# Attention in a decoder layer: the split of the output weights moved from VectorE and GpSimd to GpSimd alone, and spread over two pairs of heads

## The chip, the cores and the metric

The kernel runs on one core of a Trainium2 chip. The metric is the device time of one execution, in microseconds. TensorE is the matrix engine (its matrix products are PE in the profile, its weight loads PEld), VectorE is DVE, ScalarE is ACT, GpSimd is POOL, and SyncE (SP) only issues transfers.

## The reference, cut to what matters

The kernel computes one decoder layer: a projection of a 2048 x 1024 input, a pooling mixer and an attention beside each other, an output projection, and a gated MLP. The part in question is the attention, with 8 heads of width 64 and 16 blocks of 128 queries:

```python
z = jnp.einsum('bhqd,bhkd->bhqk', qi, kf) * scale
causal = key_pos[None, :] < q_pos[:, None]
log_1m_beta = jnp.where(causal, jax.nn.log_sigmoid(-z), 0.0)
stick = lax.cumsum(log_1m_beta, axis=3, reverse=True) - log_1m_beta
a = jnp.where(causal, jnp.exp(jax.nn.log_sigmoid(z) + stick), 0.0)
return jnp.einsum('bhqk,bhkd->bhqd', a, vf)
```

Behind it comes `mix = merged @ w_out[l]`, with `w_out` of 1024 x 1024. That product is made from two halves of each operand: a high half, the float32 value rounded to fp32r, and a low half, the rest. The weights of `w_out` are brought in and split into these halves while attention still runs, for use by the next phase.

## The kernel before, in words

The phases follow each other: values, projections, attention (`phase_attention`, from about 399 to 905 us of the profile), the output projection (`phase_mix`), the two halves of the MLP.

Attention goes over 4 pairs of heads (pair 0 to 3), each with a head 0 and a head 1. A head has 40 units, and a pair so has units 0 to 79. A unit is one block of 128 queries against up to 512 keys; block q has q // 4 + 1 units, and the one on the diagonal, which comes first, is 128, 256, 384 or 512 keys wide. Blocks 0 to 3 are units 0 to 3; units 4 and 5 are block 4, units 6 and 7 block 5, and so on. Pair 0 and pair 3 are written out, pairs 1 and 2 are a loop (`steps`, L628 to L649).

A unit passes through the engines in this way. TensorE makes the scores (`scores`, L887). ScalarE makes `beta` and the remainder from them (L749, L750). VectorE runs a scan over the remainder (L861). GpSimd multiplies `beta` with the scan's result, which gives the weight (L810). TensorE transposes the weight in blocks of 128 (`turn`, L899) and multiplies it with the values (`values`, L913). Each engine has one list of instructions in the order of the units, in which the later stages of a unit stand some steps on: at step u GpSimd makes the product of unit u - 1, TensorE transposes unit u - 4 and multiplies the values of unit u - 6. ScalarE's `beta` of unit u waits for the product of unit u - 4 (four buffers), TensorE's transposition for the product of its own unit, and VectorE's scan of the first unit of block q for the product of the last unit of block q - 2. For units kept in full precision GpSimd also sums the two halves of the values once a head (`sum_v`, L774), ahead of the product of the last unit of block 5 (units 7 and 47).

The output weights come in 16 pieces of 128 x 512 (256 KB), two in flight, into two buffers in `bridge` (`wo_f`, L609). SP issues them (L704 to L707) right after the loads of pair 0's head 1 (`load_head(0, 1)`, L701); from the third on it waits until the piece two before is split (`wo_done`). Each piece has two operations: VectorE copies it to fp32r (`high_wo`, L828 to L832), GpSimd subtracts the copy from the piece (`low_wo`, L769 to L772). `wo_part` (L673) says at which unit that happens: in pair 0 at units 40, 42, 44 and so on to 70, so in head 1. At such a step the piece stands first on both engines.

SP's list goes on only behind the 16th piece: then come the waits for the stores of the projections (`qk_out`), and then, for each head that ends, the loads of the head that will take its buffers (seven transfers, 4 MB) and the two stores of its result (L710 to L714). All transfers of this phase go through SP's queue.

Of the kernel before, what the change touches and what calls it, by code (L numbers as in the profile page):

```python
# [312 lines left out]
def head_loads(s, tiles, heads, tiles_of, pair, e):  # L313

    q_hi, q_lo, k_both, v_both = tiles_of
    half = slice(e * HEAD_DIM, (e + 1) * HEAD_DIM)
    moves = []
    for part in range(2):
        rows = slice(part * HEAD_DIM, (part + 1) * HEAD_DIM)
        moves.append((as_f32(k_both[rows, :]), s["qk"][pair + heads // 2, part, half, :]))  # L320
        for hi_lo, to in enumerate((q_hi, q_lo)):
            moves.append((as_f32(to[rows, :]), s["qk"][pair, hi_lo, half, :]))
    moves.append((as_f32(v_both[:, :, :, :]), s["v"][pair * 2 + e]))
    return moves
# [237 lines left out]
def phase_attention(nc, a, c, s, wide, bridge, retired, first_head, qk_out, mixed_out, mix_start):  # L562
# [8 lines left out]
    heads = a["d_attn"] // HEAD_DIM  # L571
    scale = HEAD_DIM ** -0.5
    lead = 8
# [6 lines left out]
    total = len(units)  # L580
    per_head = total // 2
# [5 lines left out]
    whole_before = [sum(whole[:u]) for u in range(total + 1)]  # L587
    per_pair_halved, per_pair_whole = halved_before[total], whole_before[total]
    v_sum_at = {next(u for u, x in enumerate(units) if x[0] == e and x[1] == per + 1 and x[5]): e for e in range(2)}
    with ExitStack() as stack:  # L590
# [18 lines left out]
        wo_f = bridge[:, 0:2, :]  # L609
# [8 lines left out]
        one_done, wo_hi_done, wo_done = (n.sem(x) for x in ("one_done", "wo_hi_done", "wo_done"))  # L618
        wo_in = n.sems("wo_in", 2)
# [5 lines left out]
        pairs, loads = heads // 2, 7  # L625
# [46 lines left out]

        def wo_part(i, u):  # L673

            m = (u - per_head) // 2
            return m if isinstance(i, int) and i == 0 and (u - per_head) % 2 == 0 and 0 <= m < 2 * a["kc"] else None

        with nc.Block() as block:

            @block.sync  # L680
            def _(sp):
                for sem in mixed_out:
                    sp.sem_inc(sem, 16)

                def load_head(pair, e):
                    for to, source in head_loads(s, tiles, heads, (q_hi[e], q_lo[e], k_both[e], v_both[e]), pair, e):
                        sp.dma_start(to, source).then_inc(head_in[e], 16)

                def store_head(pair, e, first=0, end=tiles):
                    sp.wait_ge(o_read, done((pair * 2 + e) * tiles + (end - 1), lead))  # L690
                    row, cols = (pair * 2 + e) * HEAD_DIM, slice(first * P, end * P)
                    sp.dma_start(s["merged"][bass.ds(a["d_pool"] + row, HEAD_DIM), cols], mixed[e][0:HEAD_DIM, cols]).then_inc(mixed_out[e], 16)
                    sp.dma_start(s["attn_low"][bass.ds(row, HEAD_DIM), cols], mixed[e][HEAD_DIM:P, cols]).then_inc(mixed_out[e], 16)

                def load_first_merged(t):
                    cols = slice(t * P, (t + 1) * P)
                    sp.dma_start(mix_start["low"][t], s["attn_low"].rearrange("(c p) t -> p c t", p=P)[:, :, cols]).then_inc(merged_in[t], 16)
                    sp.dma_start(mix_start["merged"][t], s["merged"].rearrange("(c p) t -> p c t", p=P)[:, :, cols]).then_inc(merged_in[t], 16)

                sp.sem_inc(head_in[0], 16 * loads)  # L700
                load_head(0, 1)  # L701
                for sem in retired:
                    sp.sem_clear(sem)
                for m in range(2 * a["kc"]):  # L704
                    if m >= 2:
                        sp.wait_ge(wo_done, m - 1)
                    sp.dma_start(wo_f[:, m % 2, :], wo_rows[m // 2][:, (m % 2) * BANK:(m % 2 + 1) * BANK]).then_inc(wo_in[m % 2], 16)  # L707
                for e in range(2):
                    sp.wait_ge(qk_out[e], stored(2 * (a["d_attn"] // P) * (seq // BANK) // 2, 32))
                with sp.Fori(0, heads // 2 - 1) as i:  # L710
                    for e in range(2):
                        sp.wait_ge(pv_whole_done, i * per_pair_whole + (whole_before[(e + 1) * per_head] + lead))
                        load_head(i + 1, e)
                        store_head(i, e)  # L714
                store_head(pairs - 1, 0)

                store_head(pairs - 1, 1, 0, 2)
                for e in range(2):
                    sp.wait_ge(mixed_out[e], stored(pairs, 32))
                sp.wait_ge(pv_done, halved(pairs - 1, per_head) + lead)  # L720
                sp.wait_ge(pv_whole_done, kept_whole(pairs - 1, per_head) + lead)
                for t in range(2):
                    load_first_merged(t)
                store_head(pairs - 1, 1, 2, tiles - 2)
                store_head(pairs - 1, 1, tiles - 2, tiles)
# [39 lines left out]
            @block.gpsimd  # L765
            def _(pool):
                pool.sem_inc(weight_done, lead)

                def low_wo(m):  # L769
                    k, h = m // 2, m % 2  # L770
                    pool.wait_ge(wo_hi_done, m + 1)
                    pool.tensor_tensor(wide[2 + h][:, k, :], wo_f[:, h, :], as_f32(wide[h][:, k, :]), ALU.subtract).then_inc(wo_done, 1)  # L772

                def sum_v(pair, e):  # L774

                    pool.wait_ge(head_in[e], 16 * loads * pair + 16 * loads)
                    before = whole_before[e * per_head]
                    if not isinstance(pair, int):
                        pool.wait_ge(pv_whole_done, pair * per_pair_whole + (before + lead))
                    elif pair > 0 or e:  # L780
                        pool.wait_ge(pv_whole_done, pair * per_pair_whole + before + lead)
                    pool.tensor_tensor(v_f[:, :, 0, :], as_f32(v_both[e][:, :, 0, :]), as_f32(v_both[e][:, :, 1, :]), ALU.add).then_inc(v_f_done, 1)

                def first_sum(t):
                    pool.wait_ge(merged_in[t], 32)
                    merged = mix_start["merged"][t]
                    pool.tensor_tensor(merged[:, n_pool:, :], merged[:, n_pool:, :], mix_start["low"][t], ALU.add).then_inc(first_whole, 1)

                def first_scale():
                    pool.wait_ge(mix_start["squared"], 1)  # L790
                    merged = mix_start["merged"][0]
                    pool.tensor_tensor(merged, merged, scales.unsqueeze(2).broadcast_to([P, a["kc"], P]), ALU.mult).then_inc(first_scaled, 1)

                def step(i, u, behind):
                    if in_last_head(i, u) in SUMS_AT:
                        first_sum(SUMS_AT.index(in_last_head(i, u)))
                    if in_last_head(i, u) == SCALE_AT:
                        first_scale()
                    if wo_part(i, u) is not None:
                        low_wo(wo_part(i, u))  # L800
                    if behind(weight_lag):
                        v, t = behind(weight_lag)
                        e, q, key, w, first, _ = units[v]
                        if v in v_sum_at:
                            sum_v(i if u >= weight_lag else i - 1, v_sum_at[v])
                        pool.wait_ge(beta_done, done(t, lead))
                        pool.wait_ge(stick_done, done(t, lead))
                        pool.wait_ge(turned, freed(t, weight_ring, lead))
                        at = col(q, key) + 1
                        pool.tensor_tensor(weight[v % weight_ring][:, 0:w], beta[v % stick_in][:, 0:w], stick[q % 2][:, at:at + w],  # L810
                                           ALU.mult).then_inc(weight_done, 1)

                steps(pool, step)

            @block.vector
            def _(dve):
# [8 lines left out]
                    dve.wait_ge(first_hi_done, 1)  # L825
                    dve.tensor_tensor(mix_start["lo"], mix_start["merged"][0], as_f32(mix_start["hi"]), ALU.subtract)

                def high_wo(m):  # L828

                    k, h = m // 2, m % 2  # L830
                    dve.wait_ge(wo_in[h], 16 * (k + 1))
                    dve.tensor_copy(wide[h][:, k, :], wo_f[:, h, :]).then_inc(wo_hi_done, 1)  # L832

                def step(i, u, behind):
                    if wo_part(i, u) is not None:
                        high_wo(wo_part(i, u))
                    if behind(lo_lag) and not whole[behind(lo_lag)[0]]:
                        v, t = behind(lo_lag)
                        w, pair, slot = units[v][3], i if u >= lo_lag else i - 1, halved_before[v] % wT_ring
# [4 lines left out]
                    if u < total:  # L844
                        e, q, key, w, first, _ = units[u]
# [20 lines left out]
                    if behind(read_lag) and units[behind(read_lag)[0]][5]:  # L866
                        v, t = behind(read_lag)
                        e, q = units[v][0:2]
# [1604 lines left out]
```

## Time and profile before

| what | value |
|---|---|
| median of 3 runs | 2430.19 us (2427.38 to 2430.77) |
| the profiled execution's own time | 2429.78 us |
| its span, from the first to the last instruction | 2428.0 us |
| mean granted clock of TensorE, as a share of full speed | 0.986 |
| TensorE, VectorE, ScalarE, GpSimd busy over the span | 96%, 74%, 50%, 42% |
| DMA over the span | 324.71 MB, mean 134 GB/s |

All times of rows are from one execution, counted from the first instruction. A row of the order of time has start, duration, engine, line, operation, operands, how many equal ones were merged into it (x4), and in brackets how long the engine had been idle and what released it. In the tables by stretch each engine has its busy time with the count of instructions, PEclk is the share of full clock that TensorE was granted, and the last two columns are the busy share of the DMA engines and GB/s.

### The profile page before, as it was taken

The page shows a single profiled execution, that of the slowest core. Times are in us where ns is not written, and L with a number is a line of the kernel's source. Part 1 is how long each engine was busy: PE and PEld are TensorE (multiplying, and loading weights), DVE is VectorE, ACT ScalarE, POOL GpSimd, SP SyncE. Part 2 cuts the span into 40 slices and gives each one's busy share as a digit, 9 for nine tenths or more (in the row PEclk, how much of TensorE's full clock was granted, in tenths as well). Part 3 has the DMA queues.
Part 4 walks back from the last instruction along what each step waited for, and adds up shares of the span by engine and source line. Part 5 has one row for each costly group of instructions (what it writes and reads, how often), then busy time and mean ns, then how long its engine had stood idle before and what let it go on. Part 6 is the DMA issues. An engine that isn't in the chain of part 4 may idle for free. (4 is left out here: it accounts for less than half of the span.)

```text
span 2428.0 us, 36799 instructions
## 1 busy us (share of the span) xinstructions
PE 2326.3 (96%) x11673; PEld 1948.3 (80%) x11673; DVE 1801.1 (74%) x2126; ACT 1217.8 (50%) x2114; POOL 1018.9 (42%) x758
## 2 busy tenths in 40 slices
PE   8999999989999989996999999989999999999997
PEld 6787887878888888884888888778888878888886
DVE  5434224999999977888999999999999973344575
ACT  4311114879889974555444444544444443342352
POOL 0000002776666653566454555455554521041642
PEclk9999999999999999998999999999999999999999
DMA  6412447153333325777233332633333324455584
GB/s 192 140 47 82 136 130 199 32 138 90 85 90 87 86 64 169 225 220 255 88 108 100 116 102 93 204 110 103 95 108 95 116 95 168 161 176 190 196 307 153
DMA packets 264699, 324.71 MB, mean 134 GB/s; under 512 B 12996, under 2 KB 185980, under 8 KB 259580
## 3 DMA queue, kind: packets, MB, share of 16 engines
q1 hardware_dynamic: 262268, 314.72, 41.8%
q0 software_dynamic: 2304, 8.39, 0.9%
q8 instruction: 69, 1.13, 0.2%
q14 instruction: 58, 0.48, 0.1%
HBM read 213.48 MB, written 109.58 MB: 133 GB/s over the span
## 5 line engine op out<-in xcount | busy, mean ns | idle before, releaser
L810 POOL TENSOR_TENSOR weight<-beta,stick 128x512 f32<-128x512 f32 (+3 forms) x320 | 304.8, 961 | 540.9 <-ACT beta L749 422.7
L2186 DVE SCALAR_TENSOR_TENSOR x<-up_cols,taps,x 128x1024 f32<-128x1024 f32 x174 | 263.9, 1517 | 14.4 <-ACT x L2083 11.4
L861 DVE TENSOR_TENSOR_SCAN stick<-z_ps,stick,beta 128x512 f32<-128x512 f32 x192 | 245.1, 1277 | 13.3 <-ACT z_ps L750 12.1
L535 PE MATMUL out_ps<-hT,w_hi 128*128 128x512 f32 x768 | 239.5, 393 | 2.4 <-DVEq L462 2.4
L2173 DVE TENSOR_TENSOR wu_lo<-wu_sums,wu_hi 128x512 fp32r<-128x512 f32 x175 | 213.3, 1219 | 0.0
L749 ACT ACTIVATE beta<-z_ps 128x512 f32<-128x512 f32 (+3 forms) x320 | 171.4, 536 | 57.5 <-PE z_ps L893 50.4
L2070 ACT ACTIVATE wu_hi<-wu_sums 128x512 fp32r<-128x512 f32 x175 | 109.5, 627 | 161.1 <-PE gate_odd_ps L2316 89.5
L2316 PE MATMUL value_chain_ps<-wide,wu_hi 128*128 128x512 f32 x528 | 177.0, 389 | 2.1 <-DVE up_cols L2208 2.1
L910 PE MATMUL wT_ps<-ident,weight 128*128 128x128 f32 x1088 | 173.3, 275 | 3.1 <-POOL weight L810 3.1
L535 PEld LDWEIGHTS out_ps<-hT,w_hi 128*128 128x128 f32 x768 | 145.0, 189 | 34.6 <-DVEq L462 2.8
L750 ACT ACTIVATE z_ps<-z_ps 128x512 f32<-128x512 f32 (+3 forms) x320 | 172.1, 538 | 0.0
L910 PEld LDWEIGHTS wT_ps<-ident,weight 128*128 128x128 f32 x1088 | 135.4, 141 | 32.0 <-POOL weight L810 4.8
L535 PE MATMUL out_ps<-hT,w_lo 128*128 128x512 f32 x384 | 150.2, 391 | 0.0
L2083 ACT ACTIVATE x<-up_cols,taps 128x1024 f32<-128x1024 f32 x87 | 108.4, 1246 | 78.7 <-DVE up_cols L2280 57.4
L1709 DVE TENSOR_TENSOR down_lo<-down_lo,down_hi 128x1024 fp32r<-128x1024 f32 (+1 forms) x57 | 71.7, 1264 | 95.1 <-ACT down_hi L1627 95.1
L1798 PE MATMUL down_ps<-down_hi 128*128 128x512 f32 x352 | 137.2, 390 | 1.6 <-DVE down_lo L1715 1.6
L2316 PE MATMUL value_chain_ps<-wide,wu_lo 128*128 128x512 f32 x352 | 137.0, 389 | 0.0
L1798 PE MATMUL down_ps<-down_hi,down_lo 128*128 128x512 f32 x352 | 136.9, 389 | 0.0
L1798 PE MATMUL down_ps<-down_lo,down_hi 128*128 128x512 f32 x352 | 136.9, 389 | 0.0
L921 PE MATMUL o_ps<-wT_f,v_f 128*128 128x128 f32 x1024 | 136.1, 276 | 0.0
L921 PEld LDWEIGHTS o_ps<-wT_f,v_f 128*128 128x128 f32 x1024 | 125.3, 193 | 0.0
L2316 PE MATMUL value_chain_ps<-x_t,wu_hi 128*128 128x512 f32 x352 | 111.0, 397 | 13.0 <-DVE up_cols L2287 13.0
(279 smaller groups left out, 6205.4 us busy)
## 6 DMA issues: line engine op xcount, KB each, us to landing
wu_f<-in_w_up SPq DMA_DIRECT2D x44, 512.0 KB, 4.9
bridge<-in_w_up SPq DMA_DIRECT2D x44, 512.0 KB, 5.0
f_scratch<-f_sum SPq DMA_DIRECT2D x88, 256.0 KB, 2.0
down_lo<-f_scratch SPq DMA_DIRECT2D x44, 512.0 KB, 3.4
f_scratch<-x SPq DMA_DIRECT2D x66, 256.0 KB, 2.1
down_b<-in_w_down SPq DMA_DIRECT2D x65, 256.0 KB, 3.9
x_scratch<-x SPq DMA_DIRECT2D x56, 256.0 KB, 2.8
first_head<-qk_scratch SPq DMA_DIRECT2D x24, 512.0 KB, 10.0
```

What stands on the lines that cost most here:

```text
L535: m = pe.matmul(out_ps[half + j][:, :], w[slot][:, k, :], hT[h][:, k, j * BANK:(j + 1) * BANK], start=(k == 0 and t == 0), stop=(k == kc - ...
L749: act.activation(beta[u % stick_in][:, 0:w], z_ps[u % bank_ring][:, 0:w], ACT.Sigmoid, scale=scale).then_inc(beta_done, 1)
L750: act.activation(z_ps[u % bank_ring][:, 0:w], z_ps[u % bank_ring][:, 0:w], ACT.Sigmoid, scale=-scale).then_inc(rest_done, 1)
L810: pool.tensor_tensor(weight[v % weight_ring][:, 0:w], beta[v % stick_in][:, 0:w], stick[q % 2][:, at:at + w], ALU.mult).then_inc(weight_do ...
L861: dve.tensor_tensor_scan(stick[q % 2][:, at:at + w][:, ::-1], backwards, beta[u % stick_in][:, 0:w], start, ALU.mult, ALU.bypass).then_inc ...
L910: m = pe.transpose(wT_ps[u % bank_ring][:, b * P:(b + 1) * P], weight[u % weight_ring][:, b * P:(b + 1) * P], c["ident"][:, :])
L921: m = pe.matmul(o_ps[q % 2][:, 0, :], v_f[:, key // P + b, :, :], wT_f[whole_before[u] % wT_ring][:, b, :], start=False, stop=False, skip_ ...
L1798: m = pe.matmul(ps[t][:, :], x[left][:, at:at + P], w, start=(not adds and k == 0 and j == 0), stop=(k == n_k - 1 and j == 2), skip_group_ ...
L2070: act.activation(a_hi[UP_LEFT.index(operand)], left_source(operand, e), ACT.Copy).then_inc(wu_hi_done, 1)
L2173: dve.tensor_tensor(a_lo[i], left_source(operand, e), as_f32(a_hi[i]), ALU.subtract).then_inc(wu_done, 1)
L2186: dve.scalar_tensor_tensor(out=conv[h], in0=cols[:, h, 2 - back:2 - back + span], scalar=column(kind, h, e), in1=conv[h], op0=ALU.mult, op ...
L2316: m = pe.matmul(bank[:, :], w[left][:, k, :], x[right][:, k, :], start=(not adds and k == 0 and t == 0), stop=(k == half - 1 and t == 2), ...
```

## The change: what it does

The 16 pieces are no longer split in pair 0's head 1. `wo_part` now gives piece u // 10 at units 5, 15, 25 and on to 75 of pair 0 (pieces 0 to 7), and piece 8 + u // 5 at units 2, 7, 12 and on to 37 of pair 3 (pieces 8 to 15). Both operations of a piece are GpSimd's: it waits for the piece, copies it, waits for its own copy, and subtracts; all this stands ahead of the product of unit u - 1. VectorE's part goes. SP issues pieces 0 to 5 ahead of the loads for pair 1's head 0, pieces 6 to 9 ahead of those for pair 1's head 1, and pieces 10 to 15 behind the loop, whose last pass holds the loads of pair 3's head 1 and the stores of pair 2's head 1. The sizes, the buffers and the waits for `wo_done` stay.

```diff
         def wo_part(i, u):
 
-            m = (u - per_head) // 2
-            return m if isinstance(i, int) and i == 0 and (u - per_head) % 2 == 0 and 0 <= m < 2 * a["kc"] else None
+            if isinstance(i, int) and i == 0 and u < total and u % 10 == 5:
+                return u // 10
+            if isinstance(i, int) and i == pairs - 1 and u < per_head and u % 5 == 2:
+                return a["kc"] + u // 5
+            return None
...
-                for m in range(2 * a["kc"]):
+                def load_wo(m):
                     if m >= 2:
                         sp.wait_ge(wo_done, m - 1)
                     sp.dma_start(wo_f[:, m % 2, :], wo_rows[m // 2][:, (m % 2) * BANK:(m % 2 + 1) * BANK]).then_inc(wo_in[m % 2], 16)
+
+                def next_head(i, e):
+                    sp.wait_ge(pv_whole_done, i * per_pair_whole + (whole_before[(e + 1) * per_head] + lead))
+                    load_head(i + 1, e)
+                    store_head(i, e)
+
+                for m in range(6):
+                    load_wo(m)
                 for e in range(2):
                     sp.wait_ge(qk_out[e], stored(2 * (a["d_attn"] // P) * (seq // BANK) // 2, 32))
-                with sp.Fori(0, heads // 2 - 1) as i:
+                next_head(0, 0)
+                for m in range(6, 10):
+                    load_wo(m)
+                next_head(0, 1)
+                with sp.Fori(1, pairs - 1) as i:
                     for e in range(2):
-                        sp.wait_ge(pv_whole_done, i * per_pair_whole + (whole_before[(e + 1) * per_head] + lead))
-                        load_head(i + 1, e)
-                        store_head(i, e)
+                        next_head(i, e)
+                for m in range(10, 2 * a["kc"]):
+                    load_wo(m)
                 store_head(pairs - 1, 0)
...
-                def low_wo(m):
+                def split_wo(m):
                     k, h = m // 2, m % 2
+                    pool.wait_ge(wo_in[h], 16 * (k + 1))
+                    pool.tensor_copy(wide[h][:, k, :], wo_f[:, h, :]).then_inc(wo_hi_done, 1)
                     pool.wait_ge(wo_hi_done, m + 1)
                     pool.tensor_tensor(wide[2 + h][:, k, :], wo_f[:, h, :], as_f32(wide[h][:, k, :]), ALU.subtract).then_inc(wo_done, 1)
...
                     if wo_part(i, u) is not None:
-                        low_wo(wo_part(i, u))
+                        split_wo(wo_part(i, u))
...
-                def high_wo(m):
-
-                    k, h = m // 2, m % 2
-                    dve.wait_ge(wo_in[h], 16 * (k + 1))
-                    dve.tensor_copy(wide[h][:, k, :], wo_f[:, h, :]).then_inc(wo_hi_done, 1)
-
                 def step(i, u, behind):
-                    if wo_part(i, u) is not None:
-                        high_wo(wo_part(i, u))
```

## Rows read from the trace of the kernel before

**Rows 1.** Busy time by stretch: pair 0's head 1, pair 2's head 1 (PE, PEld, DVE, ACT, POOL).
```profile
457.00:530.40 73.40, 61.51 (x433) 53.52 (x431) 67.73 (x98) 56.10 (x122) 62.35 (x59) 0.98 0.45 118
712.40:772.60 60.20, 58.40 (x435) 52.30 (x434) 57.57 (x82) 54.74 (x121) 40.38 (x41) 1.00 0.35 89
```

**Rows 2.** TensorE in order of time, over the whole of attention.
```profile
409.86 0.27 PE L910 MATMUL wT_ps<-ident,weight 128*128 128x128 f32 x1
...
413.59 0.60 PE L910 MATMUL wT_ps<-ident,weight 128*128 128x128 f32 x4
...
456.83 0.31 PE L893 MATMUL z_ps<-k_both,q_hi 128*128 128x128 f32 x1
...
477.71 0.99 PE L910 MATMUL wT_ps<-ident,weight 128*128 128x128 f32 x4 [2.09 <-POOL weight L810]
...
530.45 0.32 PE L893 MATMUL z_ps<-first_head 128*128 128x128 f32 x1 [3.32 <-DMA first_head<-v_scratch]
...
712.48 0.31 PE L893 MATMUL z_ps<-k_both,q_hi 128*128 128x128 f32 x1
...
772.71 0.30 PE L893 MATMUL z_ps<-first_head 128*128 128x128 f32 x1
...
794.54 0.60 PE L910 MATMUL wT_ps<-ident,weight 128*128 128x128 f32 x4
...
795.68 0.60 PE L910 MATMUL wT_ps<-ident,weight 128*128 128x128 f32 x4
```

**Rows 3.** The two operations of a piece by line (ns least/median/most).
```profile
L832 DVE CAST wide<-bridge x16: 399/524/1304, 458.6 to 513.1; 128x512 fp32r<-128x512 f32 x16
...
L772 POOL TENSOR_TENSOR wide<-bridge,wide x16: 1267/1282/1295, 459.1 to 513.7; 128x512 fp32r<-128x512 f32 x16
```

**Rows 4.** SP's queue in order of time, pair 0's start and pair 3's.
```profile
402.66 0.57 SPq L687 DMA_DIRECT2D v_both<-v_scratch  x1
406.32 0.82 SPq L707 DMA_DIRECT2D bridge<-in_w_out  x2
...
787.76 0.51 SPq L693 DMA_DIRECT2D attn_low_scratch<-mixed  x1
```

**Rows 5.** Issue to landing: pieces 0 and 1, pieces 2 to 15; last load, last store.
```profile
DMA to landing us min/median/max: 14.4/14.5/14.6
...
DMA to landing us min/median/max: 2.4/2.6/2.9
...
v_both<-v_scratch SPq DMA_DIRECT2D x1, 1024.0 KB, 17.5
...
attn_low_scratch<-mixed SPq DMA_DIRECT2D x1, 512.0 KB, 18.0
```

**Rows 6.** GpSimd in order of time: the kernel's start, pair 0, pair 3.
```profile
0.41 0.10 POOL L2463 MEMSET const-float32-1.0<- 128x1 f32 x1
...
0.87 0.20 POOL L161 MEMSET ident<- 128x128 f32 x1 [0.29 <-POOLq L2463]
1.31 0.29 POOL L163 TENSOR_SCALAR_AFFINE_SELECT ident<-ident 128x128 f32<-128x128 f32 x1 [0.24 <-POOL ident L161]
...
405.47 1.46 POOL L810 TENSOR_TENSOR weight<-beta,stick 128x512 f32<-128x512 f32 x2 [0.68 <-DVE stick L861]
407.64 1.69 POOL L810 TENSOR_TENSOR weight<-beta,stick 128x512 f32<-128x512 f32 x2 [0.71 <-DVE stick L861]
409.29 2.39 POOL L782 TENSOR_TENSOR v_f<-first_head 128x1024 f32<-128x1024 f32 x1
...
791.70 1.10 POOL L810 TENSOR_TENSOR weight<-beta,stick 128x512 f32<-128x512 f32 x1 [0.35 <-DVE stick L861]
```

**Rows 7.** Granted clock in three stretches (length, PE busy, PEclk, DMA share, GB/s).
```profile
399.00:410.00 11.00, 10.46 (x40) 0.53 0.93 204
476.00:480.00 4.00, 2.29 (x12) 0.74 0.07 24
480.00:484.00 4.00, 4.00 (x28) 0.84 0.20 66
```

## The prediction

> **What bounds the kernel now.** I read the busy table by stage first, then TensorE's order of time across the heads, with the gaps in it, then SP's and GpSimd's. In an undisturbed head TensorE is busy for 58.4 of 60.2 us, VectorE for 57.6, GpSimd only for 40.4 [rows 1]: TensorE sets the pace, VectorE is just behind it, and GpSimd has a third of its time free. A head begins where the 128-wide score product of unit 0 stands. Pair 2's second head runs from 712.48 to 772.71, that is 60.2 us. Pair 0's second head, which holds all 16 pieces of the output weights, runs from 456.83 to 530.45, 73.6 us [rows 2]. So the work that the change moves costs **13.4 us** today. Of it, 3.3 us is one wait of TensorE at 530.45 for the loads of the next head [rows 2]; the other 10.1 us are the pieces' own work on two engines, among them a wait for a GpSimd product ending at 477.71 [rows 2] and 16 casts on VectorE of 399 to 1304 ns each [rows 3].
>
> **What is removed.** The 16 casts on VectorE, the pieces' crowding (one every second unit), and the place of the next head's loads behind the last piece. If the second head comes back to the length of an undisturbed one, this gives all of 13.4 us. I take the whole: -13.4. The loads of pair 1's first head can leave at about unit 46, some 50 us ahead of unit 80 (34 units of 60.2/40 = 1.5 us), and such a set lands within 17.5 us of its last issue [rows 5].
>
> **What one piece costs on GpSimd.** The subtract stays at 1.28 us [rows 3]. The copy has no row. GpSimd's write-only fill of 128x128 takes 0.20 us and of 128x1 0.10, so 512 columns give at least 0.5 us; the two-input subtract of the same tile, 1.28, is the other end. The select of 128x128, which reads one input, takes 0.29 [rows 6]; above the fill's fixed 0.10 that is 0.19 us for 128 columns, so 0.86 us for 512: I take that, the nearest kind. The subtract waits for the copy on the same engine, as the select waited for the fill: 0.24 us [rows 6]. A piece is **2.4 us** (2.0 to 2.8). The Trainium skill (GPSIMD Engine Reference, Engine selection) speaks against two-input work on GpSimd and calls one-input work roughly line rate; an estimate from its 1.2 GHz makes the copy some 0.4 us and the sum 0.9 us smaller over the two pieces that count below. No row here shows it.
>
> **The first piece, pair 0 unit 5.** What decides is not that time but when the piece is there. SP issues the seven loads of head 1 (pair 0), 4 MB, up to 402.66, and only at 406.32 the first piece [rows 4]. It lands 14.4 us later, at 420.7, where a piece with nothing ahead of it needs 2.4 to 2.9 us [rows 5]. Today nobody asks for it before unit 40, at 457. Now GpSimd does: its product of unit 3 ends at 406.6 (405.47 and 1.1; units 3 and 4 stand in one row) [rows 6], and in its program the piece stands ahead of unit 4's product. Behind it are the products of units 4 to 7 and the head's value sum; TensorE's transposition of unit 4, at 409.86 today [rows 2], waits for the first of them, ScalarE and VectorE for later ones. So: landing 420.8, split done 423.2, product 4 (0.4) 423.6, products 5 and 6 (1.7) 425.3, value sum (2.4) 427.7, product 7 (1.1) 428.8 (durations of [rows 6]). Unit 7's transposition is at 413.59 today [rows 2]; it comes at 428.9. **+15.3 us.** TensorE has no slack to win that back.
>
> **The clock.** After a gap of 2.1 us ahead of 477.71 [rows 2] the granted clock was at the lower level (1.2 GHz) for 3.4 us (0.74 and 0.84 of two slices of 4 us), which loses 1.7 us; over the first 11 us of attention it was 0.53, so low for some 10 of them [rows 7], which loses up to 5 us. A gap of 13 us will bring at least one such stretch. In pair 0 part of it falls where TensorE waits for product 7 anyway: I take +1.5 (0 to 4).
>
> **The eleventh piece, pair 3 unit 12.** Its load is now issued behind the loads and stores of the last pass of SP's loop. The last of these is issued at 787.76 and lands 18.0 us later, at 805.8 [rows 4, 5]. The piece is issued just after and, at 0.6 us for 256 KB (the first two landed at 420.7 and 421.3), lands at 806.4. GpSimd would need it at 792.8, when unit 10's product ends (791.70 + 1.10) [rows 6]. Split done 808.9, product 11 810.0; its transposition is at 795.68 today [rows 2]. **+14.3 us**, and the ninth and tenth piece (units 2 and 7; the one at unit 7 meets the value sum and would by itself hold TensorE for 1.5 us) disappear inside it, as the landing goes by the queue's time. Clock after it: +3.0 (1.7 to 5), as here only TensorE bounds.
>
> **The other pieces.** They are loaded in time: SP issues pieces 2 to 5 while attention's first head runs; piece 6 near unit 46, behind 5 MB that take 18 us, for unit 65, 28 us on; the last ones two pieces ahead. (Pieces count from 0; the first is 0, the eleventh 10.) Without the load, GpSimd's time remains. Unit 10's product waits 0.35 us before it starts [rows 6] and ends 1.7 us before its transposition at 794.54 [rows 2]: 2.1 us of cover against 2.4. At 0 to 0.3 us each, more if the copy is slow: +1.0 for them together (0 to 5).
>
> **Sum.** -13.4 + 15.3 + 1.5 + 14.3 + 3.0 + 1.0 = +21.7 us. The profiled execution took 2429.8 us, so 2451.5; the median of the runs shown is 0.4 above it: **2452 us**, 0.9% slower.
>
> **Rivals.**
> (a) *Both pieces are there in time*: the small load overtakes the big ones. The Trainium skill (DMA: Bandwidth & Descriptors, Queues, rings and completion order) says that completion is not in order per issuing engine, which would allow this. Then -13.4, +1.0 at unit 7 of pair 0, +1.5 at unit 7 of pair 3, +1.0: about -10, **2420 us**, faster. Against it: the trace's own first two pieces landed after 14.4 and 14.6 us and not after 2.6 [rows 5], just behind the head's loads. 4%.
> (b) *Only one of the two stands*, for instance since SP reaches the eleventh piece earlier, or GpSimd unit 12 later, than I place them: -13.4 + 16.8 + 2.5 = +6, **2436 us**. 6%. The point from which it decides: the piece must land within 2 us of 792.8.
> (c) *The waits hold, and GpSimd and the clock are dear*: copy 1.28 us and over five us of lower clock in each stall: +0.8, +4.5 and +4 on the sum, **2461 us**. GpSimd then lags through the whole of each touched head. 12%.
> (d) *The change doesn't free the second head*: its 13.4 us were not the split's but its own. Then only the costs are left, **2465 us**. Against it: the head with the same units in pair 2 takes 60.2. 2%.
> (e) My forecast and its surroundings: 76%.
>
> **How the numbers follow.** Low ends: no clock loss in pair 0, 1.7 in pair 3, copy 0.5, nothing for the other pieces: +17. One more us off for landings: 2445; the range reaches a little further, to 2443, for parts of (b). Upward it takes in most of (c): 2460. A measurement of this kernel tells 0.2%, 4.9 us, from no change. Faster by more is (a) with a remainder, 0.05; within it is the low edge of (b), 0.03; slower is all else, 0.92.
>
> **What would show it.** In the new profile: GpSimd idle for 14 us at about 406.6 with the landing of the output weights as its releaser, TensorE idle 13 us before a transposition near 423.6, granted clock near half in the slices after; pair 0's second head back to about 60 us with no wait at its end; the same stall once more in pair 3's first head, about 18 us after its start; a GpSimd copy between 0.5 and 1.3 us. It is wrong if the first piece lands before 410, or if pair 0's second head stays above 65 us.

## The result, and the profile after

The changed kernel takes 2447.01 us (median of 4 runs, 2446.07 to 2448.42) where the kernel before, run beside it, takes 2428.82 (2427.38 to 2430.77). The ratio is 1.0075, 95% interval 1.0061 to 1.0089: 18.2 us slower. The forecast was 2452 (2443 to 2460), slower with a chance of 0.92. The profiled execution took 2446.07 us, with a span of 2444.3, which is 16.3 above the span before.

GpSimd in order of time around pair 0's unit 5 and pair 3's unit 12 of the changed kernel. L787 is the copy, L789 the subtract, L827 the product, L799 the value sum:

```profile
405.60 1.09 POOL L827 TENSOR_TENSOR weight<-beta,stick 128x512 f32<-128x512 f32 x1 [0.68 <-ACT beta L764]
420.69 0.61 POOL L787 CAST wide<-bridge 128x512 fp32r<-128x512 f32 x1 [14.00 <-DMA bridge<-in_w_out]
421.38 1.26 POOL L789 TENSOR_TENSOR wide<-bridge,wide 128x512 fp32r<-128x512 f32 x1
422.60 2.06 POOL L827 TENSOR_TENSOR weight<-beta,stick 128x128 f32<-128x128 f32 x3
424.62 2.37 POOL L799 TENSOR_TENSOR v_f<-first_head 128x1024 f32<-128x1024 f32 x1
426.94 2.98 POOL L827 TENSOR_TENSOR weight<-beta,stick 128x512 f32<-128x512 f32 x3
...
790.42 4.01 POOL L827 TENSOR_TENSOR weight<-beta,stick 128x512 f32<-128x512 f32 x4
806.38 0.61 POOL L787 CAST wide<-bridge 128x512 fp32r<-128x512 f32 x1 [11.94 <-DMA bridge<-in_w_out]
807.07 1.26 POOL L789 TENSOR_TENSOR wide<-bridge,wide 128x512 fp32r<-128x512 f32 x1
```

The bracket is what to read here. GpSimd, which had a third of its time free in [rows 1], stands still for 14.00 us and then for 11.94, and both times the releaser is the landing of a piece of the output weights. Its work on the piece is 0.61 + 1.26 us and a handover of 0.08 (421.38 less 420.69 + 0.61).

TensorE in order of time, changed kernel. These rows answer to [rows 2]: the first transposition behind either stall, unit 7's transposition, and the score products of unit 0, at which a head begins:

```profile
423.07 0.48 PE L919 MATMUL wT_ps<-ident,weight 128*128 128x128 f32 x1 [14.56 <-POOL weight L827]
428.24 0.60 PE L919 MATMUL wT_ps<-ident,weight 128*128 128x128 f32 x4
...
471.33 0.31 PE L902 MATMUL z_ps<-k_both,q_hi 128*128 128x128 f32 x1
...
531.22 0.33 PE L902 MATMUL z_ps<-first_head 128*128 128x128 f32 x1
...
773.67 0.30 PE L902 MATMUL z_ps<-first_head 128*128 128x128 f32 x1
...
809.43 0.47 PE L919 MATMUL wT_ps<-ident,weight 128*128 128x128 f32 x1 [12.04 <-POOL weight L827]
...
848.29 0.31 PE L902 MATMUL z_ps<-k_both,q_hi 128*128 128x128 f32 x1
```

| stretch, by TensorE's rows | before | after | difference |
|---|---|---|---|
| pair 0, head 0 (holds four pieces; the wait for piece 0) | 57.4 | 71.6 | +14.2 |
| pair 0, head 1 (held all 16 pieces; now 4) | 73.6 | 59.9 | -13.7 |
| pairs 1 and 2, four heads | 242.3 | 242.5 | +0.2 |
| pair 3, head 0 (holds eight; the wait for piece 10) | 60.2 | 74.6 | +14.4 |
| pair 3, head 1, to the next phase's first product | 72.0 | 70.8 | -1.3 |
| the next phase, to the first product of the one behind it | 220.3 | 223.2 | +2.9 |
| all else | | | -0.4 |

SP's queue in order of time, and behind it the issue-to-landing lines of pieces 0 and 1 and of pieces 10 and 11 (answer to [rows 4, 5]):

```profile
402.95 0.58 SPq L690 DMA_DIRECT2D v_both<-v_scratch  x1
406.63 0.82 SPq L710 DMA_DIRECT2D bridge<-in_w_out  x2
...
788.69 0.51 SPq L696 DMA_DIRECT2D attn_low_scratch<-mixed  x1
789.43 0.88 SPq L710 DMA_DIRECT2D bridge<-in_w_out  x2
```

```profile
DMA to landing us min/median/max: 14.0/14.1/14.2
...
DMA to landing us min/median/max: 16.9/17.0/17.1
```

The issues and the landings are those of the kernel before; only their reader has moved. Nothing in the old profile called piece 0 late, because nobody waited for it. The granted clock in the stretches around the two stalls (length, PE busy, PEclk, DMA share, GB/s; answers to [rows 7]):

```profile
412.00:422.00 10.00, 0.00 (x0) 0.50 0.81 231
422.00:427.00 5.00, 3.93 (x16) 0.50 0.19 56
427.00:431.00 4.00, 4.00 (x30) 0.98 0.00 0
803.00:812.00 9.00, 2.57 (x13) 0.50 0.45 170
812.00:816.00 4.00, 4.00 (x29) 0.89 0.16 50
```

TensorE came back at the lower level, 1.2 GHz, and stayed on it until about 427 in the first case and 813 in the second, 4.1 and 3.5 us behind the restarts.

### The profile page after: what moved, and what is told of

Same layout as the page of the kernel before. It is cut to its first block and busy times, and to the rows that moved or that the text cites. A ratio compares the mean times of both kernels' runs of the same rounds, so it can differ in the third digit from the quotient of the medians.

```text
span 2444.3 us, 36761 instructions
## 1 busy us (share of the span) xinstructions
PE 2324.0 (95%) x11673; PEld 1947.5 (80%) x11673; DVE 1789.9 (73%) x2110; ACT 1216.8 (50%) x2114; POOL 1024.1 (42%) x774
## 5 line engine op out<-in xcount | busy, mean ns | idle before, releaser
L827 POOL TENSOR_TENSOR weight<-beta,stick 128x512 f32<-128x512 f32 (+3 forms) x320 | 303.2, 957 | 528.8 <-ACT beta L764 429.0
L919 PE MATMUL wT_ps<-ident,weight 128*128 128x128 f32 x1088 | 172.6, 274 | 27.4 <-POOL weight L827 27.4
L870 DVE TENSOR_TENSOR_SCAN stick<-z_ps,beta 128x128 f32<-128x128 f32 (+3 forms) x128 | 103.3, 812 | 37.0 <-ACT z_ps L765 20.3
```

What stands on the lines that cost most here:

```text
L870: dve.tensor_tensor_scan(stick[q % 2][:, at:at + w][:, ::-1], backwards, beta[u % stick_in][:, 0:w], start, ALU.mult, ALU.bypass).then_inc ...
L919: m = pe.transpose(wT_ps[u % bank_ring][:, b * P:(b + 1) * P], weight[u % weight_ring][:, b * P:(b + 1) * P], c["ident"][:, :])
```

## The experiments

**One load early, two kernels.** The first moves pieces 0 and 1 ahead of the loads of pair 0's head 1. The second does the like for pieces 10 to 13, unrolls SP's loop for it, and splits pieces 14 and 15 at units 33 and 38 of pair 3 instead of 32 and 37.

```diff
+                load_wo(0)
+                load_wo(1)
                 load_head(0, 1)
...
-                for m in range(6):
+                for m in range(2, 6):
                     load_wo(m)
```

> Edit: the changed kernel with pieces 0 and 1 issued ahead of the seven loads of pair 0's head 1 instead of behind them; nothing else. Theory (GpSimd waits for a landing behind 4 MB on SP's queue): piece 0 lands within some 3 to 6 us of its issue, GpSimd does not stop at unit 5, pair 0's head 0 is back from 71.6 to about 57.5 us, and the time falls by 14 us, from 2447 to about 2433; the second stall, at pair 3's unit 12, stays at 12 us. Rival (GpSimd's added work or the copy itself holds TensorE at unit 5): the time stays within 3 us of 2447.

Measured: 2432.68 us (10 runs), 14.3 below the changed kernel. GpSimd in order of time:

```profile
405.48 1.09 POOL L829 TENSOR_TENSOR weight<-beta,stick 128x512 f32<-128x512 f32 x1 [0.68 <-issue]
406.51 0.61 POOL L789 CAST wide<-bridge 128x512 fp32r<-128x512 f32 x1
```

The copy follows the product of unit 3 with no gap, and pair 0's head 0 lasts 57.4 us, as before the change, though the work of four pieces is still in it. The 14 us were the landing alone.

```diff
-            if isinstance(i, int) and i == pairs - 1 and u < per_head and u % 5 == 2:
-                return a["kc"] + u // 5
+            if isinstance(i, int) and i == pairs - 1 and u in (2, 7, 12, 17, 22, 27, 33, 38):
+                return a["kc"] + (2, 7, 12, 17, 22, 27, 33, 38).index(u)
...
-                with sp.Fori(1, pairs - 1) as i:
+                for i in range(1, pairs - 1):
                     for e in range(2):
+                        if i == pairs - 2 and e == 1:
+                            for m in range(10, 14):
+                                load_wo(m)
                         next_head(i, e)
-                for m in range(10, 2 * a["kc"]):
+                for m in range(14, 2 * a["kc"]):
                     load_wo(m)
```

> Edit: the changed kernel with pieces 10 to 13 issued ahead of the loads of pair 3's head 1, which then wait for the split of piece 11, and pieces 14 and 15 due at units 33 and 38 of pair 3 instead of 32 and 37; pieces 0 and 1 as in the changed kernel. Theory: the stall before unit 12 of pair 3 goes, pair 3's head 0 is back from 74.6 to about 61 us, the loads of head 1 land some 10 us before unit 40, and the time is about 2433; the first stall stays. Rival (the delayed loads of head 1 now stop TensorE at unit 40): head 0 of pair 3 lasts 65 us or more and the time is above 2437.

Measured: 2435.21 us (10 runs), 11.8 below the changed kernel and 2 above the expected value. Pair 3's head 0 lasts 63.2 us: the stall before unit 12 is gone, but not all of its time. What is left is a wait of GpSimd for piece 14, 2.8 us in this profile; the next run shows the same.

**Both early.** The two edits above together.

> Edit: both of the above. Theory: neither stall; the time is the changed kernel's less 28.5 us, 2418 to 2420, that is 9 to 11 us below the kernel before, and the granted clock stays up through attention after its first 10 us. Rival (GpSimd's spread pieces cost TensorE something at every place, up to 0.3 us each): 2422 to 2425.

Measured: 2422.89 us (7 runs), ratio to the kernel before 0.9971 (0.996 to 0.9982). Faster than before, and still 3 us dearer than I expected. Whom GpSimd waited for within attention, and GpSimd in order of time:

```profile
POOL wide L792 <- DMA bridge<-in_w_out: 3.2, 1, 3.2
```

```profile
811.20 1.09 POOL L832 TENSOR_TENSOR weight<-beta,stick 128x512 f32<-128x512 f32 x1 [0.68 <-issue]
815.53 0.61 POOL L792 CAST wide<-bridge 128x512 fp32r<-128x512 f32 x1 [3.24 <-DMA bridge<-in_w_out]
```

I had made the same mistake as the change, in small: piece 14, due at unit 33, is now the one behind the delayed 4 MB of head 1 and the two stores. It was issued at 797.63 and used at 815.53. The expectation had left it out. It had also said that the granted clock would stay up. In this profile it fell once more, for 3.4 us at the start of pair 2's head 0 (0.57 from 640 to 644 us), and that head lasts 61.6 us instead of 59.9. TensorE had been idle for 1.8 us just before; but the kernel before idles 2.0 us there without a dip. The same dip stands in two other profiles (the next head's loads behind the pieces again, and the changed kernel with fills); what brings it stays open.

**No wait left.** All else as both early.

```diff
-            if isinstance(i, int) and i == pairs - 1 and u in (2, 7, 12, 17, 22, 27, 33, 38):
-                return a["kc"] + (2, 7, 12, 17, 22, 27, 33, 38).index(u)
+            if isinstance(i, int) and i == pairs - 1 and u in (2, 9, 14, 19, 24, 29, 36, 41):
+                return a["kc"] + (2, 9, 14, 19, 24, 29, 36, 41).index(u)
```

> Edit: the version with both loads early, and pair 3's pieces at units 2, 9, 14, 19, 24, 29, 36 and 41, so that none meets the value sum at unit 7 and piece 14 is due after its landing behind the 4 MB of head 1. Theory (what that version lost in pair 3 was a 3.2 us wait of GpSimd for piece 14 and 0.8 us at unit 7): pair 3's head 0 falls from 63.6 to about 60.5 us, and the time from 2422.9 to about 2420. Rival (the pieces' work itself): head 0 stays above 62.5.

Measured: 2417.58 us (5 runs), ratio to the kernel before 0.9956 (0.9942 to 0.997), 5.3 us below the version with both early where 3 were expected; pair 3's head 0 lasts 61.0 us and gives 2.6 of them. GpSimd's wait for pieces is down to 1.2 us, and TensorE waits only 2.1 us for its products in all of attention, where the changed kernel had 27.4. This version beats both kernels: 10.9 us below the one before, 29.4 below the changed one. GpSimd's spread work by itself thus costs at most about 1 us in the head with eight pieces.

**Which queue.** The changed kernel, with pieces 0 and 1 issued by ScalarE.

```diff
-                for m in range(6):
+                for m in range(2, 6):
                     load_wo(m)
...
                 for sem in (rest_done, beta_done, hi_done, whole_done):
                     act.sem_inc(sem, lead)
+                for m in range(2):
+                    act.dma_start(wo_f[:, m % 2, :], wo_rows[m // 2][:, (m % 2) * BANK:(m % 2 + 1) * BANK]).then_inc(wo_in[m % 2], 16)
```

> Edit: the changed kernel with pieces 0 and 1 issued by ScalarE at the start of attention, on its own queue, instead of by SP behind the seven loads; pieces 10 on as in the changed kernel. Theory in its strict form (the order on one queue holds the piece back): it lands within 8 us of its issue while SP's loads are still under way, and GpSimd's wait at unit 5 is gone or below 2 us; pair 0's head 0 lasts 58 to 60 us. Rival (the 16 DMA engines are full until about 420 whatever queue the piece is on): it still lands at 415 or later and the stall stays above 8 us.

Measured: 2432.58 us in a single run, pair 0's head 0 57.2 us. SP's first loads and ScalarE's two pieces, in order of time on each queue:

```profile
399.09 0.48 SPq L690 DMA_DIRECT2D k_both<-qk_scratch  x1
399.62 0.59 SPq L690 DMA_DIRECT2D q_hi<-qk_scratch  x1
...
399.17 1.14 ACTq L747 DMA_DIRECT2D bridge<-in_w_out  x2
```

The issue-to-landing lines of piece 0, of both pieces together, and of the last load of head 1 (`v_both`):

```profile
DMA to landing us min/median/max: 6.0/6.0/6.0
...
DMA to landing us min/median/max: 6.0/9.2/12.3
...
DMA to landing us min/median/max: 19.6/19.6/19.6
```

Piece 0 landed 6.0 us after its issue, and the stall is gone, as expected. The last of SP's loads landed 2.6 us later behind its issue than in the changed kernel (17.0). But this does not show that it was the order on SP's queue that held the piece. The edit also moved the issue from 406.63 to 399.17 us, ahead of all but the first of the seven loads. Piece 1 stands against the new queue as the cure: issued at 399.6, it took 12.3 us and landed at 411.9, behind two 512 KB loads of SP's, one issued at the same time (399.62, 8.4 us to landing) and one after it (400.25, 11.4 us). What the run shows is that the engines were not so full that a piece issued at the start of the burst must wait for its end. No run issues a piece late on a second queue.

**Who copies.** As both early, with the copy on VectorE again.

```diff
-                    pool.wait_ge(wo_in[h], 16 * (k + 1))
-                    pool.tensor_copy(wide[h][:, k, :], wo_f[:, h, :]).then_inc(wo_hi_done, 1)
...
+                def high_wo(m):
+                    k, h = m // 2, m % 2
+                    dve.wait_ge(wo_in[h], 16 * (k + 1))
+                    dve.tensor_copy(wide[h][:, k, :], wo_f[:, h, :]).then_inc(wo_hi_done, 1)
...
+                    if wo_part(i, u) is not None:
+                        high_wo(wo_part(i, u))
```

> Edit: as both early, but the copy of each piece is VectorE's again, at the same spread units, and only the subtract GpSimd's. Theory (VectorE is nearly the bound, so each copy of 0.4 to 0.65 us on it delays a scan): 3 to 8 us above the version with both operations on GpSimd, some 2423. Rival (spreading and early loads are the whole gain, and which engine copies does not matter): within 2 us of it.

Measured: 2425.55 us (11 runs, 2421.56 to 2430.57), 2.7 above the version with both operations on GpSimd, just short of the 3 expected, with spreads that overlap. The profile is clearer: pair 0's two heads last 59.5 and 61.6 us instead of 57.5 and 59.9, and TensorE waits longer for VectorE's low halves within attention:

```profile
PE o_ps L951 <- DVE wT L862: 17.0, 39, 1.6
```

against 12.4 us with the copies on GpSimd. But the phase behind attention took 218.7 us in it, 4.7 less than there.

**Crowded on GpSimd.** The kernel before with only the copy moved to GpSimd; pieces still at every second unit.

```diff
                     k, h = m // 2, m % 2
+                    pool.wait_ge(wo_in[h], 16 * (k + 1))
+                    pool.tensor_copy(wide[h][:, k, :], wo_f[:, h, :]).then_inc(wo_hi_done, 1)
                     pool.wait_ge(wo_hi_done, m + 1)
...
-                    dve.wait_ge(wo_in[h], 16 * (k + 1))
-                    dve.tensor_copy(wide[h][:, k, :], wo_f[:, h, :]).then_inc(wo_hi_done, 1)
```

> Edit: the kernel before with the copy moved to GpSimd and nothing else: pieces at units 40, 42 and so on to 70 of pair 0, SP's order as before. Theory (GpSimd needs 1.9 us for a piece and some 1.9 for the products of two units, in 3.1 us of TensorE's pace): GpSimd becomes the bound of that head, which lasts 75 to 79 us instead of 73.6, and the time is 2431 to 2435, slower than before. Rival (the casts on VectorE were what cost): the head is below 72 us and the time below 2427.

Measured: 2433.65 us (10 runs), ratio 1.0022 (1.0013 to 1.0031). Busy time in that head, and whom TensorE waited for in it:

```profile
457.00:532.30 75.30, 61.09 (x435) 52.71 (x433) 60.18 (x83) 56.34 (x122) 70.52 (x75) 0.98 0.43 112
```

```profile
PE wT_ps L904 <- POOL weight L812: 11.2, 13, 3.2
PE z_ps L887 <- DMA first_head<-v_scratch: 3.1, 1, 3.1
```

GpSimd is busy for 70.5 of 75.3 us and sets the pace. Moving the copy without spreading the pieces makes the kernel slower; the spreading, with the place of the next head's loads, carries the gain.

**The next head's loads behind the pieces again.** The version with no wait left, with the loads of pair 1's head 0 issued behind piece 8.

```diff
-                next_head(0, 0)
-                for m in range(6, 10):
+                for m in range(6, 9):
                     load_wo(m)
+                next_head(0, 0)
+                load_wo(9)
```

> Edit: the best version so far (no wait left), with the loads of pair 1's head 0 issued behind pieces 6 to 8 instead of ahead of them, so after unit 65's piece is split. Theory (the old place of these loads cost a wait at unit 80 and nothing else): they land some 2 to 5 us after TensorE needs them, the second head of pair 0 lasts 62 to 66 us instead of 59.9, and the time is 2 to 5 us above 2417.6. Rival (the loads were hidden anyway, and the old wait was only a part of the crowding): head 1 stays at 60 us and the time within 1 us.

Measured: 2422.24 us (5 runs). The kernel before ran 1.3 us higher beside it than beside the version it is compared with, so 3.3 to 4.7 us dearer. Unit 0 of pair 1 in TensorE's order of time:

```profile
519.54 0.32 PE L908 MATMUL z_ps<-first_head 128*128 128x128 f32 x1 [3.40 <-DMA first_head<-v_scratch]
```

The head ahead of it lasts 63.4 us instead of 59.9. This is the old 3.3 us wait, with the crowding gone.

**Fills in place of the copies.** The table's +2.9 us in the next phase has no part of the change in it. In the profiles, that phase took 223.2 to 223.6 us in all eight kernels with neither copies nor fills on VectorE, the crowded one among them, and less in the two with copies (220.3 and 218.7). So I gave VectorE back 16 instructions that do next to nothing (fills of 128x1, 0.06 us each), first in the version with no wait left, then in the changed kernel.

```diff
                 def step(i, u, behind):
+                    if wo_part(i, u) is not None:
+                        dve.memset(c["eps"][:, :], EPS)
```

> Edit: the version before this one with a fill of 128x1 on VectorE at each piece's step, 16 in all, where the old kernel had its copies; 0.06 us each. The phase behind attention took 220.3 us in the kernel before and 218.7 where VectorE copies, but 223.2 to 223.5 in all versions where GpSimd does. Theory (the place of VectorE's instructions in memory, shifted by 16 removed ones, delays that phase): it is back at 218.5 to 220.5 us and the time some 3 us below the version without fills. Rival (it is GpSimd's list, longer by 16, or something else): it stays at 223 and the time is the same or 1 us above.

> Edit: the changed kernel, with a fill of 128x1 on VectorE at each piece's step and nothing else. Theory (3 of the changed kernel's added microseconds are in the phase behind attention and hang on where VectorE's instructions lie, which the 16 removed copies shifted): that phase is back from 223.2 to 220.3 us in the profile, the two stalls stay at 14.0 and 11.9 us, and the time is 1 to 3 us below 2447. Rival (the phase's length moves by itself, or only under the profiler): the phase stays at 223 or the median does not move.

Measured: 2416.73 us (5 runs) for the first, 0.9 below the version without where 3 were expected, with overlapping spreads, so its median shows no gain; 2445.12 us (6 runs), ratio 1.0067 (1.0055 to 1.0079), for the second, 1.9 below the changed kernel by the medians and 2.9 by the distances to the kernel before. TensorE's first product of the phase and of the one behind it, changed kernel:

```profile
919.04 0.34 PE L1313 MATMUL ss_ps<-ones,x 128*128 128x1 f32 x1 [2.89 <-PEq L681]
...
1142.23 0.76 PE L2325 MATMUL gate_even_ps<-x_first,wu_hi 128*128 128x512 f32 x1 [5.97 <-DVEq L2174]
```

and the same with the fills:

```profile
920.84 0.24 PE L1315 MATMUL ss_ps<-ones,x 128*128 128x1 f32 x1 [2.89 <-PEq L681]
...
1140.15 0.77 PE L2327 MATMUL gate_even_ps<-x_first,wu_hi 128*128 128x512 f32 x1 [5.98 <-DVEq L2176]
```

223.2 us became 219.3, and 223.4 became 220.4 in the other pair. In these twelve profiles the phase is long where the 16 instructions of VectorE are missing ahead of it, and short where something stands in their place.

The trace also shows where the delay begins. The phase's loop handles two tiles in a pass, and in all eight long profiles VectorE pauses once in each pass before the same instruction, which reads the result of the one before it: 0.49 us the first time, then five times 0.23 to 0.25. In the four short ones it pauses 0.12 us there, too little for a bracket. Changed kernel, the first and the third pause; then the kernel before at the place of the third:

```profile
956.75 1.29 DVE L1268 SCALAR_TENSOR_TENSOR hn<-xo,stat_mix,bridge 128x1024 f32<-128x1024 f32 x1 [0.49 <-DVE stat_mix L1265]
...
1007.27 1.28 DVE L1268 SCALAR_TENSOR_TENSOR hn<-xo,stat_mix,bridge 128x1024 f32<-128x1024 f32 x1 [0.24 <-DVE stat_mix L1265]
...
992.67 0.16 DVE L1256 RECIPROCAL stat_mix<-stat_mix 128x1 f32<-128x1 f32 x1 [0.46 <-ACT stat_mix L1147]
992.96 1.28 DVE L1259 SCALAR_TENSOR_TENSOR hn<-xo,stat_mix,bridge 128x1024 f32<-128x1024 f32 x1
```

A transfer of 8 KB on the queue that brings instructions (q14 in the profile) starts 0.8 us behind the start of the first delayed instruction in all eight (957.52 us in the changed kernel), and some 9 us ahead of that instruction in the four short ones. This fits instructions that lie elsewhere in memory than before; no run moves them by themselves, so it is argued, not shown. Some 140 us into the phase VectorE is 0.7 us late by these pauses. How that grows to 2.9 us is not shown either: GpSimd's last addition starts that much later, 198.4 us behind the phase's first product instead of 195.5, and waits for a store of its own where it waited 6.3 us for VectorE before:

```profile
1117.46 2.35 POOL L1122 TENSOR_TENSOR xo<-xo,mix 128x1024 f32<-128x1024 f32 x1 [8.18 <-DMA x_scratch<-xo]
```

That wait is no mark of the long phase, since it stands in the changed kernel with fills too, at 6.9 us. In the median of runs this is worth 1 to 3 us, and no more can be said from these runs.

## Why the prediction was right

**What is removed, -13.4.** Head 1 of pair 0 went from 73.6 to 59.9: -13.7. Both halves of the reason hold: the loads' wait comes back alone, at 3.4 us, when the loads are put behind the pieces again, and the crowding is dear on whichever engine has it (73.6 us with the copies on VectorE, 75.4 with them on GpSimd).

**The piece's price, 2.4 us.** Measured 1.95: copy 0.61 and not 0.86, handover 0.08 and not 0.24. The copy lies nearer to the write-only fill than to the select that I went by. The Trainium skill (GPSIMD Engine Reference, Engine selection) calls one-input work roughly line rate; an estimate from its 1.2 GHz is 0.43 us for 512 columns, and the trace agrees if some 0.18 us are fixed. Its other half, that two-input work belongs on VectorE, no run here tests, since the subtract is GpSimd's in all of them. For the copy, the engine that is not the bound was the better place (by 2.7 us in the medians, with overlapping spreads, and by 1.6 to 2.1 us in each of pair 0's heads).

**The first piece, +15.3, and the clock, +1.5.** Unit 7's transposition came at 428.24, 14.65 later than at 413.59; 0.3 of this was there at the head's start. The forecast was 15.3: the piece is 0.45 shorter, and it landed 14.0 us after its issue and not 14.4. The landing itself, forecast at 420.7 and read at 420.69, is so close because the issue came 0.3 us later. The head as a whole gained 14.2 us, so the clock's term was zero here. The clock was low for 4 us behind the restart, but GpSimd worked all but without a gap from 420.69 to beyond 429, and TensorE had to go by its products.

**The eleventh piece, +14.3, and the clock, +3.0.** Landing forecast 806.4; GpSimd went on at 806.38. This agreement is luck: the head began 0.96 us later than in the old trace, and the last store ahead of the piece landed 16.9 us after its issue and not 18.0. The transposition came at 809.43, 13.75 later than at 795.68, of which 0.96 was there at the head's start: 12.8. The 1.5 us that are missing from 14.3 are this faster landing and the shorter piece. The head gained 14.4, so 1.6 us are left for the stretch at 1.2 GHz and for the pieces behind the stall together. With no stall and the same number of pieces, the head lasts 0.8 us longer than before (61.0 against 60.2), so the clock cost some 0.8 to 1.6 us (3.4 us at the lower level without a stall made pair 2's head 0 longer by 1.6), where 3.0 was taken and 1.7 was the low bound from [rows 7].

**The other pieces, +1.0.** In pair 0 the heads show nothing: head 1 with four of them lasts 59.9 us, below the undisturbed 60.2. In pair 3 they cost up to 0.8 us, as just said. At 1.95 us a piece fits into the 2.1 us of cover that the prediction read from [rows 2, 6], but not everywhere.

**Not foreseen.** +2.9 us in the next phase and -1.3 at the end of attention, where TensorE's sequencer waits 2.9 us instead of 4.2. The parts that the prediction named make -13.7 + 14.2 + 14.4 = +14.9 where +21.7 was forecast; with these two and the smaller terms the profiled sum is +16.3, and the medians' +18.2 is between the two. So some of the closeness is luck: the phase that nobody touched moved the time towards the forecast. Without these two the median would be at about 2445.4, nearer to the low end.

**The rivals.** (a), that the small load overtakes, falls: both pieces that stalled GpSimd landed behind all the loads and stores issued ahead of them. The Trainium skill (DMA: Bandwidth & Descriptors, Queues, rings and completion order) says that completion is not in order per issuing engine, and also that each transfer engine takes up its ring's descriptors in order. The trace agrees with both: in the kernel before, a 64 KB store issued 2.7 us behind a 512 KB one landed 0.5 us ahead of it (850.3 against 850.8), but half a microsecond of disorder is nothing against a 4 MB burst. (b) falls, as both stalls stood. (c) falls with the copy at 0.61 us and 4 us of lower clock behind each stall. (d) falls with head 1 at 59.9.

The change's idea was right and its placement wrong. Spreading the pieces over GpSimd's free time and freeing the next head's loads are worth 13.7 us together; two of the 16 pieces were due before they had come through the 4 and 5 MB ahead of them on SP's queue, and each gave back as much.

## What to carry to other kernels

When a consumer is moved earlier, look up when its data lands in the old trace, not how long the load takes: a load that nobody waits for shows its lateness in no list of waits. Behind every burst on a queue, name the next transfer that is due and give its due time against the landing; do so again after each repair, since the burst, once moved, has a new one behind it. Compare inserted work with the engine's gap plus its lead over the consumer, here 0.35 + 1.7 us against a piece of 1.95: it cost nothing in pair 0's heads and up to 0.8 us in pair 3's.

## What the runs showed of the hardware that was not expected

Two queues did not serve their loads in the order of issue. A 256 KB load that ScalarE issued 0.1 us behind the first of SP's 512 KB loads landed after 6.0 us. The next one, issued 0.4 us later, took 12.3 and came in behind two more of SP's 512 KB loads, one issued together with it and one 0.6 us later. SP's burst ended 2.6 us later for the two. So a second queue is no sure way past a burst; what was sure in these runs was to issue the piece ahead of it (2.7 us to landing on SP's own queue, where it needed 14.0 behind 4 MB).

A phase with no changed instruction moved by 3 to 4 us in the profiles when 16 instructions of one engine were taken away ahead of it, and came back with 16 fills of 0.06 us. It goes with a pause of 0.23 to 0.49 us before one instruction of its loop in 12 profiles of 12; the cause behind the pause stays open.
